# Issue place of the third home's down weights in a hybrid SSM / HGRN2 / mixture-of-experts decoder step

## The reference, cut to what matters

```
x = x + mix
x = x + hier_moe(rmsnorm(x, norm_ffn_w), ...)
...
def hier_moe(h, ...):
    gates = sum(one_hot(eid, N_EXPERTS) * (gw * ew)[..., None], axis=1)   # top 1 group, top 2 experts in it
    hg = einsum('nd,edf->nef', t, w_gate)
    hu = einsum('nd,edf->nef', t, w_up)
    act = silu(hg) * hu * gates[..., None]
    return einsum('nef,efd->nd', act, w_down)
...
gate = sigmoid(rmsnorm(x, norm_ple_w) @ w_ple_gate)
x = x + gate * (p @ w_ple_proj)
```

## Time and profile before

| what | us |
|---|---|
| median of 3 runs | 667.54 |
| lowest and highest of them | 665.11, 671.46 |
| the profiled execution | 664.68 |
| its span, first to last instruction | 662.9 |
| PE busy in the span | 604.2 (91%) |
| DVE, ACT, POOL busy | 298.1, 176.0, 80.8 |
| mean granted TensorE clock | 0.968 of full |

### The profile page before, as it was taken

How to read it: one execution, slowest core, us unless ns; L and a number is a source line. 1 busy time by engine, 2 the same in 40 slices (tenths; PEclk the granted TensorE clock), 3 DMA queues, 4 the chain that set the end, 5 groups by cost and what they waited for, 6 DMA issues and landing times.

```text
span 662.9 us, 8899 instructions
## 1 busy us (share of the span) xinstructions
PE 604.2 (91%) x3418; PEld 400.1 (60%) x3418; DVE 298.1 (45%) x959; ACT 176.0 (27%) x422; POOL 80.8 (12%) x101
## 2 busy tenths in 40 slices
PE   4999999999997899799999799999898987899995
PEld 2888888778585778688877343333333322344784
DVE  2588379568549899752311740100000101025663
ACT  3122328611635133536100411111011100100323
POOL 4200023320012111100000121121111111000000
PEclk9999899999999899999999899999898987999997
DMA  9834356997325656717999598999999999998001
GB/s 276 262 128 140 116 195 206 360 344 237 127 99 168 200 170 195 236 52 261 363 397 405 203 355 337 424 424 424 426 425 422 425 420 423 427 407 296 1 1 65
DMA packets 45413, 179.64 MB, mean 271 GB/s; under 512 B 3899, under 2 KB 12543, under 8 KB 37168
## 3 DMA queue, kind: packets, MB, share of 16 engines
q1 hardware_dynamic: 34848, 147.21, 56.9%
q0 software_dynamic: 10000, 30.67, 14.5%
q10 hardware_dynamic: 520, 1.15, 0.5%
HBM read 167.65 MB, written 17.39 MB: 279 GB/s over the span
## 4 chain that ended last, share of the span: by engine, by line
PE 66%; DMA 21%; DVE 8%; issue 2%; ACT 1%; SPq 1%; ACTq 0%; DVEq 0%
PE bank L897 21%; DMA arena<-in_w_exp_up 15%; PE bank L1341 11%; PE bank L1136 9%; PE bank L1377 5%; DVE arena L1803 5%; DMA arena<-in_w_in 5%; PE bank L1475 4%; PE bank L1050 2%; DVE arena L1811 2%; DVE arena L2064 1%; PE bank L1350 1%; PE bank L994 1%; PE bank L1200 1%; PE bank L1004 1%
## 5 line engine op out<-in xcount | busy, mean ns | idle before, releaser
L897 PE MATMUL bank<-hT,arena 128*128 128x264 f32 x768 | 176.9, 390 | 1.6 <-DMA arena<-in_w_in 0.9
L897 PEld LDWEIGHTS bank<-hT,arena 128*128 128x128 f32 x768 | 145.7, 192 | 27.9 <-ACT arena L1581 2.5
L1341 PE MATMUL bank<-arena,hT 128*64 128x512 f32 x512 | 121.4, 623 | 19.0 <-DMA arena<-in_w_exp_up 13.5
L1341 PEld LDWEIGHTS bank<-arena,hT 128*64 128x64 f32 x512 | 39.7, 143 | 92.0 <-issue 90.4
L1811 DVE SCALAR_TENSOR_TENSOR hT<-hT,sq,bank 128x256 f32<-128x256 f32 x16 | 7.7, 480 | 138.1 <-ACT hT L1725 138.1
L1803 DVE TENSOR_TENSOR arena<-arena 128x256 f32<-128x256 f32 (+7 forms) x146 | 60.3, 457 | 16.5 <-ACT arena L1618 9.2
L1377 PE MATMUL bank<-arena,sq 128*64 128x512 f32 x256 | 58.5, 599 | 0.9 <-ACT sq L1730 0.9
L1136 PE MATMUL bank<-arena 128*128 128x264 f32 x256 | 58.1, 387 | 1.1 <-issue 1.1
L1136 PEld LDWEIGHTS bank<-arena 128*128 128x128 f32 x256 | 48.4, 190 | 10.1 <-issue 2.1
L1548 ACT ACTIVATE arena<-bank 128x264 f32<-128x264 f32 x40 | 15.5, 389 | 111.9 <-PE bank L897 111.8
L1725 ACT ACTIVATE hT<-bank 128x256 f32<-128x256 f32 x16 | 6.1, 383 | 143.0 <-PE bank L1341 143.0
(11 more groups left out here) (310 smaller groups left out, 671.9 us busy)
## 6 DMA issues: line engine op xcount, KB each, us to landing
arena<-in_w_exp_gate SPq DMA_DIRECT2D x16, 2048.0 KB, 25.1
arena<-in_w_exp_up SPq DMA_DIRECT2D x16, 2048.0 KB, 29.5
arena<-in_w_exp_down SPq DMA_DIRECT2D x16, 2048.0 KB, 20.9
arena<-in_w_in SPq DMA_DIRECT2D x13, 2048.0 KB, 10.2
out<-arena POOLq DMA_DIRECT2D x18, 512.0 KB, 5.6
arena<-in_w_out SPq DMA_DIRECT2D x4, 2048.0 KB, 11.2
arena<-in_state_ssm POOLq DMA_DIRECT2D x8, 512.0 KB, 8.1
arena<-in_state_hgrn POOLq DMA_DIRECT2D x8, 512.0 KB, 5.9
```

The lines of the kernel that those rows point to most:

```text
L897: last = mm(ps[:, 0:T], w[:, k, j * P:(j + 1) * P], x, start=(k == 0), stop=(k == KT - 1))
L1341: last = mm(bank[p][r, :].rearrange("p (w f) -> p w f", w=2), xgT[:, p, k % 4, CAP * (k // 4):CAP * (k // 4) + CAP], gu[:, :, k, FF // 2 * ...
```

## The change

The wait for the first gather moves behind the issue of expert 2's down weights. SyncE issues them as soon as the token rows have landed in DRAM, and waits for the gather only before the embedding's weights.

```diff
             eng.wait_ge(hrow_out, 48)
+            load_down(2)
             eng.wait_ge(main.rows[0], 16)
-            load_down(2)
             ple_weights(ld_pp)
```

## The result

The changed kernel takes 672.49 us (median of 20 runs, 668.69 to 677.97) against 667.86 us for the kernel before (20 runs, 664.83 to 672.49). The two medians lie 4.6 us apart; the ratio, which is that of the means, is 1.0062 with a 95% interval of 1.004 to 1.0085: 4.1 us slower, between 2.7 and 5.7. The forecast was 669.6 us, with a range of 665.5 to 674.0. The profiled execution took 672.55 us, with a span of 670.8 us against 662.9; it lies at its kernel's median, that of the kernel before 3.2 us under its own, so the two spans differ by more than the runs do.

A forecast was written before the change was run, and what follows sets the result against it. The prediction took the end to be set by a full weight stream that starts when TensorE ends expert 0's down. Median 667.54 plus 2.1 us of waiting for the gather, gain nothing, gave 669.6 us; range 665.5 to 674.0.

The forecast's parts named there:

- What bounds the kernel: The end hangs on the full weight stream, starting at 404.60 us when TensorE ends expert 0's down.
- The issue and the gather: SyncE issues the load at 376.2 us; expert 0's gather takes 6.9 us; TensorE waits 2.1 us at L1350.
- The 3 us of waiting: TensorE's wait if one packet held all of a DMA engine's share of the load; time 670.5 us.
- The gain of the moved bytes: Expert 2's down weights landing earlier: costed at nothing, since nobody waits for those loads.
- The clock: TensorE's clock may fall after the wait, making gate and up of expert 0 take 1.5 us more.
- the likeliest sum: TensorE's 2.1 us wait for the gather, clock holding, on the median 667.54: 669.6 us.
- a case of its own: Rival: 2.1 us wait at expert 0 plus 1.5 us from the clock's fall, 3.6 us, 671.1 us; chance 0.26.
- the clock that holds: Forecast case: gather late by about 3.5 us, TensorE waits 2.1 us, clock holds, 669.6 us; chance 0.42.
- The free 1.3 us: Slack between the gather's landing at 380.9 us and TensorE's need of it at 382.27 us (L1350).
- The faster rival: The 2 MB moved into the still spot leave the full stretch: end 5.0 us earlier, 662.5 us; chance 0.06.
- the signs of being wrong: Gather landed by 382.2 us, DMA full at 400 to 405 us, or end and stream start moving by different amounts.
- The clearly slow rival: Gather takes 10.5 us, TensorE waits 5.7 us, clock stays at half: 9.0 us, 676.5 us; chance 0.07.

The follow-up runs named there:

- e4_delay: Kernel before, its own order of loads, with GpSimd clearing a buffer six times more so the first gather begins about 3.6 us later; ratio 1.0058.
- e10_after: The changed kernel, unedited, executed once more; gate and up of expert 0 took 8.75 us.
- e3_more: Changed kernel with the embedding's weights (1.25 MB) also issued ahead of the wait for the first gather; ratio 1.0052.
- e1_half: Changed kernel with only half (1 MB) of expert 2's down weights ahead of the wait for the first gather; ratio 1.0001.
- e6_swap_early: Changed kernel with down of expert t issued behind gate and up of expert t; ratio 1.0059.
- e7_earlier: Changed kernel with expert 2's down weights issued still earlier, ahead of the wait for the stored token rows; ratio 1.011.
- e8_before: The kernel before, unedited, executed once more; gate and up of expert 0 took 7.09 us.
- e9_before: The kernel before, unedited, executed again; gate and up of expert 0 took 8.78 us.
- e5_swap: Kernel before with down of expert t issued behind gate and up of expert t, from expert 4 on; ratio 0.996.
- e2_warm: Changed kernel with two more filler matmul pairs on TensorE between the first table and expert 0's turned rows; ratio 1.0013.

## Why the prediction was right

**What bounds the kernel: right.** The end hangs on when the full stream begins, and that on TensorE's end of expert 0's down. Both moved by 6.2 us between the two profiles, and in e4_delay, where no load was moved, expert 4's down went out 7.7 us later than before (412.29) and the last up weights of the chain landed 8.0 us later (588.6). Not all of that is the gather's: the index (L1218) began 1.05 us later in the changed kernel's profile and 2.57 us later in that of e4_delay, with nothing changed ahead of it. One reading of the chain was off without harm: it holds three loads of up weights of over 30 us, not two (one more, of 33.72 us, begins at 498.85).

**The issue and the gather: right, nearly to the number.** SyncE issues the load 0.8 us later than the 376.2 that I took, less than the 1 us by which this execution was behind already. The gather takes 6.8 us; I had 6.9, from the gather of expert 1 beside the same load. The wait at L1350 is 2.37 us (2.18 in e10_after) where I had 2.1. That 1.25 MB more behind the load cost only 0.3 us (e3_more) and half the load nearly nothing (e1_half) fits a gather that waits for what stands at the head of the other queue. By the rule of the Trainium skill (DMA: Bandwidth & Descriptors, section on queues, rings and completion order) a DMA engine turns to another queue only after a whole packet. The 3 us of waiting that I worked out under that rule, with a packet as large as a DMA engine's whole share of the load, were an estimate. The runs agree with its kind and came out below it (2.37 and 2.18 us), since the gather landed with the load and not 1 us behind it. They don't show the rule's unit: the gather's packets began with some 200 of the load's about 256 packets through, and the views do not tell whether each DMA engine had ended its own share by then.

**The gain of the moved bytes: nothing, as costed.** e4_delay shows it by its equal loss, to within some 2.7 us, and e6_swap_early shows no gain under the other order.

**The clock: the mis-sized term.** I wrote of its fall "I don't count it in the likeliest sum and keep it for the range", with 1.5 us in a case of its own that I gave 0.26 against 0.42 for the clock that holds. It should have been in the sum. Gate and up of expert 0 took 10.04, 8.75, 9.63, 9.56 and 9.99 us in the profiles of five kernels or executions that wait there (the changed kernel, e10_after, e3_more, e4_delay, e7_earlier), 9.6 us on average; and 7.09, 7.09, 8.78, 8.78 and 7.09 us in five that don't (before, e8_before, e9_before, e1_half, e5_swap), 7.8 us on average. The difference is about 1.8 us, over what the kernel before pays there already; with the 2.3 us of waiting that makes 4.1 us. That it meets the runs' 4.1 to the tenth is luck, with so few profiles. The time from the start of the index (L1218) to the issue of expert 4's down weights divides the loss without the mixer's spread:

| profiles | us |
|---|---|
| no wait, clock holds: the kernel before, e8_before | 29.05, 28.94 |
| no wait, clock falls: e9_before, e1_half | 30.56, 30.57 |
| wait filled by matmuls, clock holds: e2_warm | 31.11 |
| wait, clock falls: e10_after, e4_delay, the changed kernel, e3_more | 33.12, 34.17, 34.26, 34.53 |

The wait alone makes 2.1 us, the fall alone 1.6 us, and both together 4.1 to 5.5 us. The likeliest sum, 2.1 us, lies outside the measured 2.7 to 5.7 us; the case next to it, 3.6 us, lies inside, and it is the one that came. The range held the time because it had been drawn around that case too.

I also read the clock of the kernel before from one execution, in which it held. Two of the five profiles without a wait show that it does not always.

**The rivals.** The free 1.3 us did cover a load half the size (e1_half), but not the whole one. The faster rival fell with the stretch of 410 to 411 us, where DMA is still again. By the letter, two of the signs of being wrong came: DMA is full at 400 to 405 us in the new profile (1.01 at 404 to 405), and the span grew by 7.9 us where the start of the stream moved by 6.2. The first had named a place by its time, and that place, ahead of expert 4's down weights, moved with expert 0's down; the second is expert 14's longer gate and up. The stream's start was forecast 2 us later and came 5.2 later, counted from the index: 2.1 of it the wait, the rest the clock. The clearly slow rival came about in another way in e7_earlier, where 3.8 us of waiting and a long fall of the clock made 7.3 us.

## What to carry to other kernels

A still spot of the DMA engines right ahead of a small transfer that the slowest chain waits for is not free room: a 2 MB load put there doubled the landing time of the gather behind it, while half the load fitted into the slack. Before moving a load forward, find out whether the end waits for its bytes at all; here a later wait on another engine restarts the stream from empty queues, so nothing sent before it could count. What paid, by 2.7 us, was to take that wait out of the way of loads that did not need it (e5_swap). And a wait can cost more than its length: here the matmuls behind it ran at half the clock, and matmuls that nobody reads, put into the wait, kept the clock up (e2_warm).

## What was not expected of the hardware

A gather that meets a load of another queue does not wait for that queue's whole content, and neither does it slip through. With the load issued about 1.5 us ahead of it each time, the first gather took 3.4 us (nothing in front), 3.9 us (1 MB), 6.8 us (2 MB) and 7.1 us (2 MB and 1.25 MB behind it). That is not in proportion to the bytes, since the load has a head start. With nothing in front, the gather's first packets move 1.8 us after its start (kernel before). By that time 0.66 of the 1.05 MB had moved in e1_half, 0.61 of the 2.10 MB in the changed kernel, and 0.59 of them in e3_more. What was left of the load at the head takes 0.9, 3.5 and 3.5 us at 426 GB/s, an estimate; the gathers took 0.5, 3.4 and 3.7 us longer.

TensorE's granted clock went from 2.4 to 1.2 GHz under expert 0's gate and up without any wait for the gather (8.78 us in e9_before and e1_half; in both the engine had idled 0.61 us ahead of the table and 0.69 us ahead of gate and up), and it fell in every profile with 2.2 to 3.8 us of waiting before them (8.75 to 10.04 us). The same instructions in the same unchanged kernel took 7.09 us in two other executions, so one profile is not enough to say what the clock does at a place like this.
